# Preparing two attention stages early: the band bias, the first rows and values, and the sample loads move into the stage ahead of them

## The reference, cut to what matters

```
x = x + 0.5 * SwiGLU_1(RMSNorm(x))
p = RMSNorm(x) @ w_in                      # 1024 -> q, k, v of A; q, k, v of B; indexer q, k, w
o_A = softmax(q k^T / 8 + rel_bias[clip(dist)] within 9 chunks of 64) v         # 8 heads x 64
isc = sum_h relu(q_idx k_idx^T) * w_idx ;  keep the 256 best keys of each query  # indexer
o_B = softmax(q k^T / 8 over the kept keys) v                                    # 8 heads x 64, rotary
x = x + concat(o_A, o_B) @ w_out
x = x + 0.5 * SwiGLU_2(RMSNorm(x)) ;  y = RMSNorm(x)
```

## Time and profile before

| | us |
|---|---|
| time before, median of 3 runs | 2753.87 (2752.5 to 2754.03) |
| the profiled execution, its own time | 2753.02 |
| its span, first to last instruction | 2751.4 |
| PE busy | 2598.3 (94% of the span) |
| DVE busy | 1353.6 (49%) |
| ACT busy | 983.5 (36%) |
| POOL busy | 512.7 (19%) |

### The profile page before, as it was taken

The page is one execution under the profiler, slowest core; times in us unless marked ns, Lnnn a source line. Parts: engine busy times, 40 slices in busy tenths (PEclk is TensorE's granted clock), DMA queues, the critical chain, the costliest instruction groups (busy, mean ns, idle before and its releaser), DMA issues. The chain is left out here.

```text
span 2751.4 us, 40367 instructions
## 1 busy us (share of the span) xinstructions
PE 2598.3 (94%) x16684; PEld 2327.1 (85%) x16684; DVE 1353.6 (49%) x2437; ACT 983.5 (36%) x1666; POOL 512.7 (19%) x368
## 2 busy tenths in 40 slices
PE   6999999999998999976999979989799999999997
PEld 6999999988878799975877766658799999998886
DVE  6433232345554598986778723332732323333554
ACT  6333323234432313133666532221533333333432
POOL 0233333200001112831000010000044343410000
PEclk9999999999999999998999989999899999999999
DMA  3122222266632122213001335550122212136553
GB/s 123 49 81 65 87 68 85 86 250 227 216 117 72 51 81 66 81 52 125 28 28 32 116 109 187 179 192 39 62 75 70 81 64 81 64 140 217 210 200 122
DMA packets 153109, 294.28 MB, mean 107 GB/s; under 512 B 14032, under 2 KB 90456, under 8 KB 152928
## 3 DMA queue, kind: packets, MB, share of 16 engines
q1 hardware_dynamic: 146688, 268.12, 28.9%
q0 software_dynamic: 6240, 23.59, 2.3%
HBM read 237.26 MB, written 61.78 MB: 109 GB/s over the span
## 5 line engine op out<-in xcount | busy, mean ns | idle before, releaser
L803 DVE TENSOR_TENSOR f_dl<-f_raw_d,f_dh 128x2048 fp32r<-128x2048 f32 x66 | 151.3, 2293 | 271.6 <-ACT f_dh L619 271.6
L619 ACT ACTIVATE f_dh<-f_raw_d 128x2048 fp32r<-128x2048 f32 x66 | 126.5, 1917 | 319.2 <-PE f_pV L151 279.7
L569 ACT ACTIVATE f_gh<-f_pX 128x256 f32<-128x256 f32 x120 | 49.3, 411 | 318.1 <-PE f_pX L151 318.1
L2088 PEld LDWEIGHTS t_po<-t_v,t_pT 128*128 128x128 f32 x1056 | 133.1, 192 | 27.5 <-issue 9.8
L1941 ACT ACTIVATE t_sc<-t_sc,t_small 128x640 f32<-128x640 f32 (+8 forms) x136 | 99.9, 735 | 152.2 <-DVE t_small L1869 117.7
L150 PE MATMUL f_pX<-f_xop,f_u_shi 128*128 128x256 f32 x504 | 149.2, 296 | 0.0
L151 PE MATMUL f_pX<-f_xop,f_u_slo 128*128 128x256 f32 x504 | 149.2, 296 | 0.0
L149 PE MATMUL f_pX<-f_xop,f_u_shi 128*128 128x256 f32 x504 | 149.2, 296 | 0.0
L149 PE MATMUL w_pw<-i_hi,r_T_hi 128*128 128x256 f32 (+1 forms) x504 | 144.6, 287 | 2.6 <-PEq L351 2.6
L150 PE MATMUL w_pw<-i_lo,r_T_hi 128*128 128x256 f32 (+1 forms) x504 | 144.8, 287 | 0.0
L151 PE MATMUL w_pw<-i_hi,r_T_lo 128*128 128x256 f32 (+1 forms) x504 | 144.2, 286 | 0.0
(11 more groups left out here) (372 smaller groups left out, 8126.5 us busy)
## 6 DMA issues: line engine op xcount, KB each, us to landing
f_raw_d<-in_ffn_w_down SPq DMA_DIRECT2D x66, 1024.0 KB, 5.0
hid<-f_gh SPq DMA_DIRECT2D x22, 1152.0 KB, 9.0
f_raw_h<-hid SPq DMA_DIRECT2D x66, 384.0 KB, 5.6
f_g_raw<-in_ffn_w_gate SPq DMA_DIRECT2D x21, 1024.0 KB, 5.3
f_u_raw<-in_ffn_w_up SPq DMA_DIRECT2D x21, 1024.0 KB, 6.5
proj<-w_stage POOLq DMA_DIRECT2D x12, 1152.0 KB, 5.6
i_raw<-in_w_in SPq DMA_DIRECT2D x12, 1024.0 KB, 5.2
f_x<-in_x_prompt SPq DMA_DIRECT2D x16, 512.0 KB, 6.7
```

The costliest lines, as they stand in the source:

```text
L569: act.activation(dst, by_tile(pX[:, c, 0:N[c]]), ACT.Copy).then_inc(s_copy, 1)
L619: act.activation(d_hi[slot(q)][:], raw_d[slot(q)][:], ACT.Copy).then_inc(s_dhi, 1)
L803: dve.tensor_tensor(d_lo[slot(q)][:], raw_d[slot(q)][:], d_hi[slot(q)][:].bitcast(F32), ALU.subtract)
L2088: last = pe.matmul(po[:, h * HD:(h + 1) * HD], pT[:, g % 2, j * P:(j + 1) * P], v[x][:, k0 + j, h * HD:(h + 1) * HD], start=j == 0, stop=j ...
```

## The change

In the in-projection:

- The bias is made there. SP loads the raw rows (`raw_b`) once DVE has read all index scores (`s_free`), POOL makes the exchange matrix (`flip`) after its last weight subtraction, PE flips after group 103 (the fifth of the last chunk), ACT alone copies the near columns and fills the far ones, POOL writes the two masked corners.
- SP loads the first rows and the first values at the end of its list. POOL no longer waits for the last two stores; SP waits for them in the attention, ahead of the second values.
- `EARLY` is 13 and the last pair starts after group 93. Every pair is spread as: query a, four heads, four heads and query b, four heads, four heads. The split of the next tile's query on DVE (`dve_expand_q`) moves from ahead of a tile's scores to the middle of them.

In the attention: rows and bias are there at the start; the copy of tile 6's scores comes after the second head; the samples' bias flip and the four row transposes are put among group B's heads (`LATE_AT`), with their DMAs, and the first two items' cached keys and values are loaded while group B runs. After the last head the sample items follow at once.

```diff
-EARLY = 16
-KEYS_AT, PAIRS_AT = 5, (8, 48, 91)
+EARLY = 13
+KEYS_AT, PAIRS_AT = 5, (8, 48, 93)
...
+            for j, keys in enumerate(([("q", a)], [(a, h) for h in range(4)], [(a, h) for h in range(4, IH)] + [("q", b)],
+                                      [(b, h) for h in range(4)], [(b, h) for h in range(4, IH)])):
+                place(at_group + j, keys, len(keys))
+        place(NT * (NCHUNK - 1) + 4, ["flip0", "flip1"], 2)
...
+            sp.wait_ge(s_free, 1)
+            sp.dma_start(raw_b[:], bass.AP(urel.tensor, FAR, [[1, P], [6 * P, H], [1, NEAR]])).then_inc(s_rel, 16)
...
+                sp.dma_start(head.rows[:, j, :], proj_v[:, 0, (1 - j) * H * HD:(2 - j) * H * HD]).then_inc(head.s_row, 16)
...
+            sp.dma_start(head.v[:], proj_v[:, 0:NP, 2 * H * HD:3 * H * HD]).then_inc(head.s_v, 16)
...
-            for i in range(2):
-                pool.wait_ge(s_put[i], 16 * NCHUNK // 2)
...
+                if h == 4 and then in tile_no:
+                    dve_expand_q(dve, then)
...
-                    if t + 1 in tile_no:
-                        dve_expand_q(dve, t + 1)
...
+LATE_AT = {(1, 4, 6): ("sb", 0), (1, 5, 1): ("sk", 0), (1, 5, 6): ("sq", 0), (1, 6, 6): ("sk", 1), (1, 7, 3): ("sq", 1)}
...
+                if n == NP + 3:
+                    sp.wait_ge(s_mx, NP * H)
...
+                    sample_rows(0)
...
+                    for s in range(2):
+                        cached_keys(s)
+                        cached_values(s)
```

More of the change, by code:

```diff
@@ L1123, in wi_phase @@
         s_rdy = [sem(f"stage_ready{i}") for i in range(2)]
-        s_put = [sem(f"stage_stored{i}") for i in range(2)]
+        s_put = head.s_put
+        s_free, s_flip, s_far = sem("index_rows_free"), sem("flip_ready"), sem("far_bias")
         s_tab = sem("tables_loaded")
@@ L1477, in pe_index @@
                     last = turn(g * P, kspread[:, 4 * g:4 * g + 4, :].rearrange("p b f -> p (b f)"))
+            elif key in ("flip0", "flip1"):
+                i = int(key[4])
+                pe.wait_ge(s_rel, 48)
+                pe.wait_ge(s_flip, 2)
+                for j in range(2):
+                    last = pe.matmul(out[:, j * 512:(j + 1) * 512], flip[:],
+                                     raw_b[:, 4 * i + 2 * j:4 * i + 2 * j + 2, :].rearrange("p h c -> p (h c)"), start=True, stop=True)
             elif key[0] == "q":
@@ L1577, in attn_phase @@
         flip_s = keep("flip_s", [P, H, DEC_S], F32)
-        at_big = keep.at
-        rows = keep("rows", [P, 2, FW], F32)
         qT = keep("qT", [P, 2, H, P], F32)
         kT, v = [None, None], [None, None]
[L1582 to L1589, removed]
+        smp = Plan(nc, tag, keep.at)
+        kT[0], kT[1] = keep("kT0", [P, HT, SEQ], F32), keep("kT1", [P, HT, SEQ], F32)
+        v[0], v[1] = head.v, keep("v1", [P, NP, FW], F32)
+        at_v0 = keep.at
+        assert at_v0 <= at_end(NP * FW * 4 + 2 * FW * 4 + 384)
         kc = [smp(f"kc{i}", [P, PAST // P, FW], F32) for i in range(2)]
-        vc = [smp(f"vc{i}", [P, PAST // P, FW], F32) for i in range(2)]
         vn = [smp(f"vn{i}", [DEC_S, FW], F32) for i in range(2)]
@@ L1670, in attn_phase @@
                 order += [(("o",) + e[1:], 1)]
-        order += [((("sk", "sq")[j], x), 0) for x in range(2) for j in range(2)]
+            elif e[0] == "late":
+                order += [(e[1:], 0)]
         order += [(("so", s), 1) for s in range(len(items))]
@@ L1870, in _ @@
                     done += n // P
[L1871 removed]
+                    if g == 1:
+                        dve.tensor_copy(acc6[:], acc[0][:]).then_inc(s_sel, 1)
+                        n_sel[0] = 1
+                    while halves and g >= 1 and (n_halves - len(halves) + 1) * todo <= n_halves * done:
                         select_half()
```

224 lines of the change are left out of this document (126 added, 98 removed).

## The result

| | before | after |
|---|---|---|
| median of 4 runs each, us | 2753.95 (2752.5 to 2758.99) | 2731.62 (2730.82 to 2736.07) |
| profiled execution, its span, us | 2753.02, 2751.4 | 2731.63, 2730.0 |

The ratio is 0.9918, 95% interval 0.9905 to 0.993: 22.3 us faster. The forecast was 2722.5 with a range of 2713 to 2734. The direction and the range held, but the median lies 9.1 us above the forecast, so nearly a third of the expected gain is missing. Against the profiled execution the forecast was -31.3 us, and the spans differ by -21.4. The ledger says where the rest is. Each line is a difference of two rows of a trace, after less before. The start of the index keys' rotation on DVE is where the part that the change touches begins.

The account below looks back on a forecast made before the run. PE was taken to set the pace beside the heads, with two seams where it idles. Terms -5.5, -14.5, +3.5, -14.8 sum to -31.3; 2753.02 + 0.85 - 31.3 = 2722.6, rounded to 2722.5 us; range 2713 to 2734.

Parts of the forecast that it names:

- term 2: Attention's opening, from its start to the third maximum: rows and bias already there, -14.5 us (bounds -13.2 and -15.5).
- term 4: From the prompt's last values to the sample items: cached keys follow at once, -14.8 us (bounds -13.5 and -16).
- The two seams: Stretches where PE idles: between in-projection and attention, and between the prompt's heads and the sample items.
- the short price: Attention's opening: copying tile 6's scores aside is short with POOL idle, giving -14.5 us; without that, -13.2.
- Term 1: End of the in-projection: three fewer DVE rounds let the next stage start earlier, -5.5 us (bounds -8 and 0).
- the end of the sums: In-projection, last pair: DVE's sums end at 1224, against 1222.5 before, with 1219 and 1228 as bounds.
- Rival (a): In-projection's end: DVE's sums end the full 5.6 us later, eating the three rounds' 6.9; 2728 us, chance 0.16.
- Term 3: Group B's heads: five more PE units and six more DVE halves, +3.5 us (bounds +2.5 and +9.7).
- A growth of more than 6 us: Sign of being wrong: the attention's own stretch grows by more than 6 us.
- (b): Group B: sample loads in SP's queue delay tile 4's rows, a stall of 11 us; 2733.5 us, chance 0.11.
- (c): In-projection's end: a late load at the end of SP's list holds the barrier; 2742.5 us, chance 0.03.
- (d): In-projection's last two chunks: flip and waiting heads keep PE's clock low, making it slower; 2773 us, chance 0.02.

Follow-up runs that it names:

- e5: The changed kernel with all three index pairs placed as before the change, the last from group 91; 2736.53 us, ratio to before 0.9929.
- e8: The changed kernel with the transposes of the sample's first key rows at head 4 of tile 5 instead of head 1; 2729.48 us, ratio 0.9905.
- e1: The changed kernel with the in-projection's last store issued by SP, with its own semaphore, instead of POOL; 2728.43 us, ratio 0.9903.
- e7: The changed kernel with only the first two index pairs placed as before the change; 2730.54 us, ratio 0.9909.
- e11: The changed kernel with the next tile's query expanded ahead of a tile's sums, as before the change; 2727.55 us, ratio 0.9888.
- e4: The changed kernel with all 16 rounds of the last selection back in the in-projection; 2736.19 us, ratio 0.9927.
- e6: The changed kernel with the last store on SP, the sample's first keys at head 4 of tile 5, and 12 rounds kept; 2727.46 us, ratio 0.9897.
- e3: The changed kernel with the transposes of the sample's first key rows at head 3 of tile 5 instead of head 1; 2730.35 us, ratio 0.9909.

## Why the prediction was right, and where it was not

*What bounds, and term 2 and term 4: right.* The two seams were the place to look (on the page of before they are its 19th and 24th slices, with PE at 6 and 7 tenths and the granted clock at 0.8, and not the 18th and 23rd), and they gave 14.5 + 15.6 = 30.2 us where I forecast 29.3. The copy aside took the short price (0.62 us against 2.61), which decided between -14.5 and -13.2. Term 4 is 0.8 larger: the cached keys come 1.5 us after the last values and not 1.9, and from them to the first score it is 5.5 us at a granted clock of 1.00, where it was 6.6 and I had taken 0.6 off. That last half is luck in part: in e5 to e8, which ran on another chip than the other experiments, the clock fell there too (0.75 to 0.80 on average), and term 4 would have been 0.9 to 1.0 us smaller.

*Term 1: wrong by 5.3 us, in two steps.* The first is "the next stage starts 0.9 us after DVE's end". I read the 0.9 us between 1259.56 and 1260.45 as what follows DVE, while the block's line shows POOL's DRAIN there until 1260.2: both engines were level, but POOL was the last. I then took POOL out of the sum with its wait. It cost 3.2 us (4.09 against the 0.9 of the sum), and e1 shows it: without POOL's store the stage ends 0.50 us after DVE. The Trainium skill, Perfetto Trace Analysis, section "DMA Instruction — SWDGE (GPSIMD)", says that the end of such a row is the writing of the last descriptor and not the landing; here the row ends at 1256.93, the landing is at 1261.5, and the DRAIN ends behind it. Had I opened the block's line in the trace of before, the 1.05 us behind the wait would have been a hint that a DRAIN is there at all; its length without the wait no row of before shows. The second step is the end of the sums, mis-sized by 2.0 us: the first round starts 353.9 us after the rotation's start, where 1224 is 351.9. POOL's subtraction held DVE's sums as I said (the second sum took 6.18 us and ended 1.0 us after it), only one sum got in ahead of it, and PE got 5.6 us back (from ACT's copy of group 89 to its last it is 77.5 us, 3.6 of them the flip, where it was 79.5) where I took 5 and 3.4. But the subtraction itself came 2.4 us later after the rotation (322.0 against 319.6). I had 1.5 us for the finer spread at the first pair, and e7 shows no gain from the old spread there. What I had at nothing was the expansion of the queries in the midst of the sums: without it DVE ends at 381.5 (e11), where my sum has 382.0 and the changed kernel 384.0. Rival (a) gave the right total for this term for another reason: DVE did end 3.4 us sooner, and another wait took it.

*Term 3: +6.6 for +3.5, inside its bounds, mis-sized in two places.* A growth of more than 6 us was one of the prediction's own signs of being wrong, and this one came. Of the 6.6 us 1.3 are the wait at `pm`, and 1.3 the slow stretch that came behind it in this execution (e8, e11). No part of my sum had them: I counted each unit's 0.60 us and not the buffer that it needs and that ACT has to have emptied. The halves are 1.6 us, not 0.5 (e4). What is left, 2.4, would be the units' own time, which I had at 3.0; it is a remainder that no run isolates. "PE is hidden from nearly all" of the halves was true of the average and false at the tiles' seams.

*The other rivals.* (b) did not come: SP issued tile 4's rows at 1451.46, behind the 4 MB, and they were due at 1461.29. They landed late, but in time, the second at 1460.10; median time to landing in a window around them and, for comparison, from 1300 to 1430:

```profile
a_rows<-proj SPq DMA_DIRECT2D x2, 256.0 KB, 7.1
```

```profile
a_rows<-proj SPq DMA_DIRECT2D x14, 256.0 KB, 2.9
```

So loads behind the 4 MB were later by 4 us, and the slack was 10; of it 1.2 us were left. The rule cited with this rival is on the order in which descriptors are consumed, which no row here shows. The order of landing was another: the first of the two rows landed at 1457.43, ahead of the last megabyte of cached values (1458.81), which was issued before it. (c) did not come: SP was done at 1231.8. (d) did not: the last chunk ran at a granted clock of 1.00.

*The range* held because it took in rivals (a) and (b), not because their mechanisms came.

## What to carry over

Taking a wait away at a stage's end is worth the distance to the next thing that ends there, and the engine's own closing DRAIN is one of those things: read the block's line on every engine, and put the last store on an engine whose DRAIN does not wait for it. Work that fits into an engine's idle share still needs a place in its queue: ask for each piece which result stands right behind it and who waits for that, and which single buffer it needs. Keeping the selection's halves off the tiles' seams gained 7.3 us against e6, a slow stretch of e6 included.

## What the runs showed of the hardware

- POOL's DRAIN at the end of a stage took 6.11 us from the issue of its own store, ending 0.55 us after the landing, 1.05 us behind an explicit wait for that store, and 2.08 us when it began under two fills and no own store was in flight. SP's took 0.12 us directly behind the same store. That POOL's DRAIN waits for the landing itself, and not for something else that ends with it, is inferred from these four: in all seven kernels without the wait and with the store on POOL the DRAIN took 6.11 to 6.12 us and the store landed after 5.5, so that a fixed time after the issue would fit as well.
- Behind PE waits of 1.08 and 1.10 us in the midst of dense work the granted clock fell in four kernels (mean 0.72 over 5 us in the changed kernel) and stayed at 1.00 in three with the same waits at the same place. It fell behind a wait of 1.49 us in e6 (0.66), and not behind one of 1.06 us in e3. At `pm` the slower stretch cost about as much again as the wait. What decides whether it comes is not shown.
- At the sample's start PE waits 1.02 us for the last output. From the last values to the first sample score it took 7.06 to 7.07 us in nine kernels with the change, and 7.95 to 8.07 in e5 to e8, where the clock fell behind that wait. The stretch from the cached keys to the first score in e8, with a granted clock of 0.75:

```profile
1598.00:1604.30 6.30, 6.01 (x34) 4.55 (x33) 2.77 (x4) 2.93 (x5) 1.19 (x6) 0.75 0.24 34
```
